# Attention's opening on one Trainium2 core: masks in three transfers, loads and gate stores in another order; second bias tables and three weight splits at other places

## The reference

```python
u = h @ w_in
q, k, v, p_in, c_in, g_in = _split_in(u)
# per head: 10 tiles of 128 queries
s_loc = q . k (window) * scale + bias, NEG_INF outside the columns of the window
s = concatenate([s_loc, q . k_ctx * scale])
p = softmax(s);  o = p_loc @ v + p_ctx @ v_ctx
y_a = o @ w_oa
gates = sigmoid(g_in + b_gate)           # 3 x 1024 columns
merged = gates[0] * y_a + gates[1] * y_b + gates[2] * y_c
x = x + gate1 * (merged @ w_out)
```

## Time and profile before

| | us |
|---|---|
| median of 3 runs | 1901.01 (1898.45 to 1901.82) |
| the profiled execution | 1899.69 |
| its span | 1897.8 |
| PE busy in it | 1859.0 (98%) |
| ACT, DVE, POOL busy | 752.6, 1152.8, 540.4 |
| mean granted TensorE clock | 0.993 of full |

### The profile page before, as it was taken

One profiled execution on the slowest core, in us unless ns is written; L12 is line 12 of the kernel. 1 busy time (PEld: TensorE's weight loads), 2 busy tenths in 40 slices (PEclk: granted clock), 3 DMA queues, 4 the chain that ended last, 5 costly groups with the idle time before them and its releaser, 6 DMA issues.

```text
span 1897.8 us, 27112 instructions
## 1 busy us (share of the span) xinstructions
PE 1859.0 (98%) x10100; PEld 1593.1 (84%) x10100; DVE 1152.8 (61%) x2150; ACT 752.6 (40%) x1435; POOL 540.4 (28%) x407
## 2 busy tenths in 40 slices
PE   8999999799999999999999999999999999999998
PEld 3788888688888888888888888888888888888898
DVE  4799996156666565356317845554443344789984
ACT  5612232255555555344313332222222222445464
POOL 0000000355554553144532144344444441000000
PEclk9999999899999999999999999999999999999999
DMA  8472535445444442656541132322222223866665
GB/s 315 158 223 61 153 120 189 117 107 127 116 113 115 121 116 61 225 162 183 183 139 59 34 124 74 95 95 73 73 73 73 73 70 119 300 206 221 217 204 207
DMA packets 243828, 260.53 MB, mean 137 GB/s; under 512 B 51057, under 2 KB 182641, under 8 KB 242673
## 3 DMA queue, kind: packets, MB, share of 16 engines
q1 hardware_dynamic: 243696, 258.80, 44.1%
HBM read 196.09 MB, written 62.65 MB: 136 GB/s over the span
## 4 chain that ended last, share of the span: by engine, by line
PE 80%; DVE 9%; DMA 3%; issue 2%; POOL 2%; ACT 2%; SPq 1%; POOLq 0%; ACTq 0%; DVEq 0%
PE ps_all L152 59%; PE ps_all L2432 4%; PE ps_all L2434 4%; PE ps_all L2433 4%; PE ps_all L1293 2%; PE ps_all L1307 2%; DVE mod_acc L817 1%; DMA wmod_then_mixers<-w_mod_dram 1%; PE ps_all L1281 1%; DMA branch_and_gates<-branch_dram 1%; PE ps_all L1284 1%; DVE X L2930 1%; DVE X L2924 1%; DVE AL L2934 1%; POOL VV L1510 1%
## 5 line engine op out<-in xcount | busy, mean ns | idle before, releaser
L152 PE MATMUL ps_all<-AH,w_hi 128*128 128x512 f32 (+1 forms) x1376 | 496.6, 361 | 13.7 <-ACT gate_rows L1352 11.3
L152 PE MATMUL ps_all<-AH,w_lo 128*128 128x512 f32 (+1 forms) x1376 | 485.2, 353 | 0.0
L152 PE MATMUL ps_all<-AL,w_hi 128*128 128x512 f32 (+1 forms) x1376 | 485.0, 352 | 0.0
L152 PEld LDWEIGHTS ps_all<-AH,w_hi 128*128 128x128 f32 x1376 | 261.7, 190 | 46.9 <-issue 11.9
L152 PEld LDWEIGHTS ps_all<-AH,w_lo 128*128 128x128 f32 x1376 | 261.5, 190 | 36.5
L152 PEld LDWEIGHTS ps_all<-AL,w_hi 128*128 128x128 f32 x1376 | 262.2, 191 | 30.4
L2998 DVE TENSOR_TENSOR quarter<-ps_all,quarter 128x512 f32<-128x512 f32 x140 | 96.5, 690 | 175.9 <-PE ps_all L152 173.9
L2852 POOL TENSOR_TENSOR slot_lo<-w_pair,slot_hi 128x512 fp32r<-128x512 f32 x96 | 130.4, 1383 | 176.0 <-ACT slot_hi L2628 176.0
L152 PE MATMUL ps_all<-AH,slot_hi 128*128 128x256 f32 (+1 forms) x384 | 129.6, 337 | 2.3 <-DVE hidden L2969 2.3
L152 PE MATMUL ps_all<-AL,slot_hi 128*128 128x256 f32 (+1 forms) x384 | 129.2, 336 | 0.0
L152 PE MATMUL ps_all<-AH,slot_lo 128*128 128x256 f32 (+1 forms) x384 | 129.1, 336 | 0.0
(11 more groups left out here) (305 smaller groups left out, 4084.5 us busy)
## 6 DMA issues: line engine op xcount, KB each, us to landing
w_raw<-w_in_dram SPq DMA_DIRECT2D x42, 512.0 KB
w_pair<-w_gu_dram SPq DMA_DIRECT2D x20, 1024.0 KB, 5.4
hidden_in<-hidden SPq DMA_DIRECT2D x77, 256.0 KB, 3.5
wmod_then_mixers<-w_mod_dram SPq DMA_DIRECT2D x19, 1024.0 KB, 7.8
hidden<-quarter SPq DMA_DIRECT2D x50, 256.0 KB, 2.1
branch_and_gates<-gates SPq DMA_DIRECT2D x16, 768.0 KB, 4.4
w_down_rows<-w_down_dram SPq DMA_DIRECT2D x44, 256.0 KB, 3.7
gates<-gate_rows SPq DMA_DIRECT2D x42, 256.0 KB, 2.0
```

Source lines behind the costliest of these rows:

```text
L152: mm = nc.tensor.matmul(out, w, a[:, k, cols[0]:cols[1]], start=(first and part == 0), stop=(last and part == 2))
```

## The change

In the opening of attention the 24 mask transfers (16 partitions each) become three of 128 partitions, which read the same 16 mask rows eight times; SP's order of keys, weights, bias, gate stores, queries and values is another. On POOL the tables of the second half of a head's bias are made at tile 1 of that head and not at tile 9 of the head ahead of it, and those of the first half one tile later. On ACT in the rear, the split of unit 23 is two branches earlier, and that of unit 24 comes after `gate_out(66)` and not after `gate_out(68)`.

```diff
--- before.py
+++ after.py
@@ -1208,20 +1208,19 @@
 
             sp.wait_ge(*front.ends[0])
             for group, kind in ((0, 0), (1, 1), (3, 2)):
-                for r in range(TROWS):
-                    sp.dma_start(col_mask[r * TCOLS:(r + 1) * TCOLS, kind, :],
-                                 g.d["col_mask"][group * TCOLS:(group + 1) * TCOLS, COL0[group]:COL0[group] + WCOLS]).then_inc(mask_in, 16)
+                sp.dma_start(col_mask[:, kind, :], mask_rows(g, group)).then_inc(mask_in, 16)
             load_k(0)
             load_w(2)
-            for half in range(2):
-                load_b(0, half)
-            for q in range(2):
-                store_gate(q)
+            store_gate(0)
+            load_b(0, 0)
+            store_gate(1)
             load_q(0)
+            store_gate(2)
+            load_b(0, 1)
             load_v(0)
             for s in range(STEPS_END + 1):
                 for q in chunks_ending(s - 1):
-                    if q >= 2:
+                    if q >= 3:
                         store_gate(q)
                 if s == 0:
                     load_w(3)
@@ -1525,7 +1524,7 @@
                 nc.gpsimd.tensor_scalar(pr[:, a:PCOLS], pr[:, a:PCOLS], c[:, 5:6], 1.0, ALU.mult, ALU.mult).then_inc(normal, 1)
 
             lower(1)
-            pool.wait_ge(mask_in, 16 * KINDS * TROWS)
+            pool.wait_ge(mask_in, 16 * KINDS)
             for half in range(2):
                 nc.gpsimd.memset(bias_src[:, half, :, :], NEG).then_inc(b_cleared, 1)
             prepare("k", 0)
@@ -1543,18 +1542,25 @@
                 for u in units_freed(s - 1):
                     if 0 < u <= BESIDE - 2:
                         lower(u + 2)
+                if n == 1 and 0 < h < HEADS:
+                    tables(h, 1)
                 if h + 1 < HEADS:
                     if n == 3:
                         prepare("k", h + 1)
-                    elif n == 5:
+                    elif n == 6:
                         tables(h + 1, 0)
                     elif n == 9:
                         prepare("v", h + 1)
-                        tables(h + 1, 1)
 
         return Engines(sync, tensor, scalar, vector, gpsimd,
                        [(g_free, 3 * BESIDE), (g_free, 3 * BESIDE - 1), (summed_v, STEPS)] + [(exp_ready, STEPS)] * 2
                        + [(p_lo[0], HEADS * NL), (p_lo[1], STEPS), (summed_v, STEPS)])
+
+
+def mask_rows(g, group):
+
+    mask = g.d["col_mask"]
+    return bass.AP(tensor=mask.tensor, offset=mask.offset + group * TCOLS * GW + COL0[group], ap=[[0, TROWS], [GW, TCOLS], [1, WCOLS]])
 
 
 def rpb_rows(g, h, first):
@@ -2715,15 +2721,17 @@
             split(BESIDE + 1)
             for n in range(KD):
                 split_branch(n)
-                if n in (3, 4):
+                if n == 2:
+                    split(BESIDE + 2)
+                elif n in (3, 4):
                     gate_out(Q0 + n - 3)
                 elif n == 5:
                     gate_out(Q0 + 2)
-                    split(BESIDE + 2)
-            for q in range(Q0 + 3, Q1):
+            gate_out(Q0 + 3)
+            split(GATES)
+            for q in range(Q0 + 4, Q1):
                 gate_out(q)
-                if q % 3 == 2:
-                    split(q // 3 + 2)
+            split(GATES + 1)
             for q in range(2):
                 open_gates(q)
             for q in range(MERGED):
```

## The result

The changed kernel took **1889.18 us** (median of 4 runs, 1888.94 to 1890.45), the kernel before beside it 1901.41 (1898.45 to 1902.35): 12.2 us less, and a ratio of 0.994 [0.9922, 0.9957], so 0.6% faster. The forecast was 1885.3 in a range of 1880.5 to 1893. The profiled execution took 1889.16, its span is 1887.3, the mean granted clock 0.995.

What follows compares the result with a forecast made beforehand. PE was taken as the bound, busy 1859.0 of 1897.8 us. Opening 12.3, tables 2.6 and rear 0.8 sum to 15.7 us, giving a forecast of 1885.3 from the median 1901.01, range 1880.5 to 1893.

Steps and rivals of the forecast that it cites:

- Opening: Start of attention: second scores 13.2 us sooner of 15.4 possible; 12.3 us in the sum, 11.6 to 12.9.
- masks: SP's opening: three wide mask transfers at 0.46 us each, 1.4 in all, so keys go out 9.66 us sooner.
- the keys' landing: Opening: ACT's `KA` starts 5.72 us after the keys' issue, at 344.35.
- the 0.7 us of spare time at piece 3: Opening: piece 3 could begin at 346.55, PE arrives at 347.26, so the first wait is gone.
- The queries' part: Opening: queries go out when `KB` ends, near 349.4, 10.6 us sooner; `gate_out(3)` is hidden by 1 us.
- The one wait that remains: Opening, second scores: PE waits 2.2 us for ACT's first exponential, behind `gate_out(5)` and `store_gate(3)`.
- the 0.9 us set aside: Opening: middle allowance for half clock (1.58 us) or a second exponential 0.3 us late behind the remaining wait.
- Second half's tables to tile 1: Attention, POOL: the five waits for scaled probabilities go, 2.6 us; tightest head keeps 2 us of cover.
- rival 3: Slower: tables at tile 1 make each `turn` late in all seven heads, 1911.2 us; chance 0.03.
- First half's tables by a tile: Attention, POOL: the shift by a tile has three tiles of room; no term in the sum.
- Splits: Rear, ACT: `split(24)` runs near 798.6, 9 us ahead of need, so PE's wait goes: 0.8 us.
- Rival 1: Keys still late in the opening, by dearer masks or later landings: total gain 11.8 us, 1889.2; chance 0.19.

Runs made afterwards that it cites:

- half0_tile5: The changed kernel with the first half's tables back at tile 5, all else as changed; 1883.54 us, ratio 0.9908 to the kernel before.
- open_only: The kernel before with the new opening alone (three wide mask transfers, SP's new order); 1888.35 us, ratio 0.9935.
- next2: half0_tile7 with unit 3's weight load and gate piece 3's store issued ahead of the values; 1881.31 us, ratio 0.99 to the kernel before.
- no_tables: The changed kernel with both halves of the tables back at tiles 5 and 9, opening and splits kept; 1885.81 us, ratio 0.9907 to the kernel before.
- tables_only: The kernel before with POOL's two table moves alone (first half to tile 6, second to tile 1 of the next head); 1907.26 us, ratio 1.0029.
- half0_tile7: The changed kernel with the first half's tables at tile 7 instead of 6; 1882.83 us, ratio 0.9895 to the kernel before.
- half0_unread: The changed kernel with heads 1 to 7's first-half tables replaced by nine fills that read nothing, their bias left out; 1881.90 us, ratio 0.9892.
- splits_only: The kernel before with the two weight splits in the rear moved, nothing else; 1896.94 us, ratio 0.9984.
- before_again: The kernel before, unchanged, run again for a second profile of its own; 1901.51 us.

## Why the prediction was right, and where it was not

The time fell in the range and in the direction forecast, but 3.9 us above the forecast of 1885.3; the mechanism of the opening was right, one step on the tables was wrong. That the time is in the range is in part luck: two errors of opposite sign stand in it. The tables at tile 6 cost 5.6 us (1889.18 against 1883.54 of half0_tile5), which the forecast had at nothing, and the other terms were together some 1.8 us too small (half0_tile5 against 1885.3).

- **Opening: right in mechanism and sum, not in its parts.** 13.2 us sooner at the second scores was forecast and is what the two profiles show, and open_only by itself is worth 12.3 us, the term of the sum. Beneath that, masks took 0.67 us each, not 0.46, and the keys' landing 6.63 us from issue to use, not 5.72. So the 0.7 us of spare time at piece 3 were gone and PE waited 0.74. The queries' part made it up: before, `QS` of head 0 ran beside POOL's tables and took 3.54 us; after, all but ahead of them, 1.78 (356.04 to 357.82, the tables from 357.40). This was in the trace of before, and was read past:

```profile
365.15 3.32 POOL L1518 TENSOR_TENSOR bias<-bias_src,col_mask 128x384 f32<-128x384 f32 x3
```
```profile
365.90 3.54 DVE L1421 SCALAR_TENSOR_TENSOR QS<-kq_src,QS 64x256 fp32r<-64x256 f32 x5 [31.28 <-ACT QS L1340]
```

- **The one wait that remains: right.** It is at the second scores, for ACT's exponential behind `gate_out(5)` behind `store_gate(3)`; 1.13 us rather than 2.2 (though with the 0.74 us ahead of it, 1.9 together). next2, which takes that store ahead of the values, has none. The clock stayed full, so the 0.9 us set aside for it were hardly spent: PE's later waits for the exponential at L1280 sum to 0.6.
- **Second half's tables to tile 1: right**, 2.7 us against 2.6 (no_tables and half0_tile5). PE did not become late at tile 1 in any head, so rival 3 as it was put, with tile 1 as its place, did not occur.
- **First half's tables by a tile: the step that failed.** "The shift of the first half by a tile has three tiles of room" asked only when the result is needed. The sum has this move at nothing. It did not ask what else runs at tile 6. DVE's `QS` of the next head runs there, and by tables_only, half0_tile5, half0_tile7 and half0_unread together it is this meeting that costs some 6 us. The Trainium skill (SBUF — State Buffer, section Who interferes with whom) has the rule: a VectorE instruction with two inputs in SBUF contends with a GpSimd instruction that reads SBUF, not with one that only writes it. `QS` has two such inputs; the runs agree, 3.04 us beside tables, 1.78 beside memsets. The trace of before had shown the conflict as well (3.54 us at 365.90, 3.55 at 551.95, against 1.78 at 456.34, alone), without any rule. What it would cost PE could not be read from these rows alone: behind 551.95 PE did not wait. For that, the work that PE has ahead of tile 8's scores in each head had to be looked at too.
- **Splits: right mechanism, a term too small.** 0.8 us was one profile's wait; others have 1.2, 1.9 and 3.2, with 1.6 us of half clock behind the 1.9, and splits_only gained 3.0 by its ratio. `w_hi` of unit 24 is made at 789.77 in the changed kernel, well ahead of PE's first product of it at 801.24, and no wait shows in any of the eight profiles with the new places.
- **Rivals.** Rival 1 gave 1889.2, and 1889.18 was measured, but its cause is not what happened: in its place is the price of tile 6. The forecast's own terms, with that one corrected, are half0_tile5: 1883.54.

## What to carry to other kernels

When an instruction is moved, look not only at when its result is due but at what runs on the other engines at the new place, and find rows of the same operation there and elsewhere: a group whose longest row is twice its shortest (`QS` 3.54 and 1.78 us) names a conflict that a move can cause or cure. GpSimd work that reads SBUF belongs beside something other than VectorE work with two SBUF inputs. A wait that shows once in one profile is a sample, not a price; where a step rests on it, look at a second profile.

## What the runs showed of the hardware

- VectorE with two inputs in SBUF and GpSimd that reads SBUF held each other off by whole instructions: the longest single `QS` operation took 2.43 us (684.38 in the changed kernel) and ended 0.3 us behind POOL's 2.40 us for a weight's lower part, where the shortest takes 0.41. POOL loses as well, but less: in the changed kernel three tables took 3.11 to 3.49 us beside `QS` and 2.94 alone.
- The TensorE clock behind an idle time of about 2 us met either level, and the length of the idle time did not decide it: half after 2.13 us in the first profile of the kernel before, full after 1.67, 1.96 and 2.06 us at the same place in before_again, splits_only and tables_only; half after 1.89 us in the rear of before_again, where the first products still ran at full, and after 2.34 in the rear of tables_only (the first product took 0.79 us); after 2.56 us full in the changed kernel and half, a microsecond later, in tables_only. So a row's first product can be short and the clock fall all the same. A wait of this length can't be given a price in advance to better than the 1.6 us between the two.
- A wait for POOL's scaling in head 0, which the profile of before did not have, is not the change's: 0.94 us at 387.39 in the changed kernel and 1.07 in half0_tile5, but also 0.33 in before_again and 1.06 in splits_only, whose opening is the old one. next2 has none there; which of its moves does that was not taken apart.
- Three mask transfers that write 128 partitions were issued in 0.67 us each, against 0.46 for those of 16 partitions. It was the same in every kernel that has them and whose row was read (1.98 to 2.03 us for three).
